# Attention inputs turned from the unscaled residual, with the inverse root applied as the projections leave PSUM

## The reference, cut to what matters

```
x  = x + rwkv7_time_mix(...)                     # ... @ w_out_a
kv = rms_norm(x, norm_kv) @ w_kv                 # k1, v1 (1024 columns each)
h  = rms_norm(x, norm_b);  proj = h @ w_in_b     # q1, gate g1 (1024 columns each)
k, q = partial_rope(rms_norm(k, k_norm)), partial_rope(rms_norm(q, q_norm))
o  = softmax(q k^T / 8, causal) v;   x = x + (o * silu(gate)) @ w_out_b
# rms_norm(x, g) = x * rsqrt(mean(x*x) + 1e-6) * g
```

## Time and profile before

| what | value |
| --- | --- |
| three runs, median (lowest to highest) | 1215.3 us (1212.01 to 1216.09) |
| the profiled execution | 1210.92 us, its span 1209.1 us |
| busy, share of the span: TensorE, VectorE, ScalarE | 92%, 60%, 41% |
| chain that ended last: TensorE, VectorE, ScalarE | 75%, 15%, 5% |
| mean granted TensorE clock | 0.977 of full |

### The profile page before, as it was taken

How to read it: one execution, slowest core, us unless ns; L and a number is a source line. 1 busy time by engine, 2 the same in 40 slices (tenths; PEclk the granted TensorE clock), 3 DMA queues, 4 the chain that set the end, 5 groups by cost and what they waited for, 6 DMA issues and landing times.

```text
span 1209.1 us, 19666 instructions
## 1 busy us (share of the span) xinstructions
PE 1113.5 (92%) x8524; PEld 900.8 (74%) x8524; DVE 730.5 (60%) x1128; ACT 501.2 (41%) x776; POOL 33.3 (3%) x30
## 2 busy tenths in 40 slices
PE   3999978898999988999998899999899699999997
PEld 2885468896768765777657699999567566998996
DVE  4671777856659956453566767667435736564544
ACT  3311313123454464345353455455233435555442
POOL 0000004400000010000000000000000000000000
PEclk9999989999999998999998999999999989999999
DMA  9373300520357450353332577866634445565520
GB/s 386 132 287 139 139 1 3 211 73 26 125 200 260 157 209 2 140 201 120 130 142 105 190 298 265 299 271 232 256 139 166 186 145 200 182 236 209 185 94 35
DMA packets 15078, 204.88 MB, mean 169 GB/s; under 512 B 1800, under 2 KB 1800, under 8 KB 2832
## 3 DMA queue, kind: packets, MB, share of 16 engines
q1 hardware_dynamic: 14256, 201.33, 44.4%
q10 hardware_dynamic: 736, 2.30, 0.5%
HBM read 202.57 MB, written 1.05 MB: 168 GB/s over the span
## 4 chain that ended last, share of the span: by engine, by line
PE 75%; DVE 15%; ACT 5%; DMA 3%; issue 2%; ACTq 0%; SPq 0%; DVEq 0%
PE bank L432 15%; PE bank L434 15%; PE bank L433 15%; PE bank L391 6%; PE bank L677 5%; PE bank L479 5%; PE bank L536 3%; DVE slot_parts L1727 3%; DMA ring<-in_stream 2%; PE bank L506 1%; ACT page_parts L1176 1%; DVE arena L1841 1%; PE bank L659 1%; ACT arena L1269 1%; DVE small L1701 1%
## 5 line engine op out<-in xcount | busy, mean ns | idle before, releaser
L432 PE MATMUL bank<-page_parts 128*128 128x512 f32 (+1 forms) x1152 | 394.1, 342 | 14.2 <-DVE page_parts L1760 9.5
L1727 DVE TENSOR_TENSOR slot_parts<-ring,page_parts 128x2048 fp32r<-128x2048 f32 x104 | 236.9, 2289 | 129.2 <-ACT page_parts L1176 128.9
L1176 ACT ACTIVATE page_parts<-ring 128x2048 fp32r<-128x2048 f32 x104 | 197.4, 1908 | 144.5 <-PE bank L434 97.5
L432 PEld LDWEIGHTS bank<-page_parts 128*128 128x128 f32 x1152 | 220.6, 191 | 39.8 <-issue 14.1
L434 PE MATMUL bank<-page_parts 128*128 128x512 f32 x576 | 227.1, 394 | 0.0
L433 PE MATMUL bank<-slot_parts,page_parts 128*128 128x512 f32 x576 | 227.0, 394 | 0.0
L1235 ACT ACTIVATE arena<-bank 128x512 f32<-128x512 f32 (+1 forms) x142 | 78.6, 570 | 223.8 <-PE bank L479 66.6
L433 PE MATMUL bank<-page_parts 128*128 128x256 f32 x576 | 163.2, 283 | 0.0
L434 PE MATMUL bank<-page_parts,slot_parts 128*128 128x256 f32 x576 | 163.2, 283 | 0.0
L434 PEld LDWEIGHTS bank<-page_parts 128*128 128x128 f32 x576 | 109.6, 190 | 23.4
L433 PEld LDWEIGHTS bank<-slot_parts,page_parts 128*128 128x128 f32 x576 | 110.1, 191 | 21.8
(11 more groups left out here) (272 smaller groups left out, 1155.1 us busy)
## 6 DMA issues: line engine op xcount, KB each, us to landing
ring<-in_stream SPq DMA_DIRECT2D x95, 2048.0 KB, 8.3
arena<-in_x SPq DMA_DIRECT2D x2, 512.0 KB, 6.3
gn<-in_gn ACTq DMA_DIRECT2D x2, 512.0 KB, 8.5
out<-arena SPq DMA_DIRECT2D x2, 512.0 KB, 2.6
cc<-in_consts ACTq DMA_DIRECT2D x1, 898.0 KB, 6.2
pc<-in_params ACTq DMA_DIRECT2D x1, 287.5 KB, 7.3
gn<-in_head_sel ACTq DMA_DIRECT2D x1, 32.0 KB
pos_i<-in_positions ACTq DMA_DIRECT2D x1, 1.0 KB, 7.1
```

Of the source, the lines that this page charges most:

```text
L432: mm(out, a[0], b[0], start=start, stop=False)
L1176: act(unit_parts(n)[0], unit_values(n)[1], ACT.Copy).then_inc(ac.step("w_hi"), 1)
L1727: tt(unit_parts(n)[1], lo, hi, ALU.subtract).then_inc(dv.step("w_lo"), 1)
```

## The change

TensorE turns X itself as soon as `add_to_x` has let each half go. ScalarE copies the eight tiles of `hkvT` first and then those of `hbT`, and forms the squares and the root afterwards. VectorE splits `hkvT`, one weight unit, `hbT`, and then forms the inverse root alone (no `XN` is written). ScalarE applies it, as a per-partition `scale`, in the 16 copies of k1, q1, v1 and g1. TensorE's direct panel there is gone; its columns are now a summed panel (eight VectorE operations) in the mLSTM stage, with its place in the order of loads after v2. The hunks below stand in the order TensorE, ScalarE, VectorE.

```diff
-            def transposes(name, src, tiles=KT, ready=None):
+            def transposes(name, src, tiles=KT, ready=None, added=None):
...
+                    if added:
+                        for tb in range(TB):
+                            pe.wait_ge(*evacuated((added, i // 2, tb)))
...
-            ada_direct()
-            pe.wait_ge(sem("xn"), 4)
-            transposes("hT_b", XN)
-            ada_turned()
+            transposes("hT_b", X, added="wo_a")
...
-                              wait=("hT_b_split", 0) if name == "k1" and half == 0 else None)
+                              wait=("hT_b_split", 4 * src) if name in ("k1", "q1") and half == 0 else None)
...
                 split_tok(("v2", half), split_parts(MLSTM_PAGES), first_of(6, 14, 11))
+            ada(1, rest=1)
             pe.wait_ge(sem("gate_rows"), 1)
...
-                               kw.get("func", ACT.Copy)).then_inc(ac.frees(product), 1)
+                               kw.get("func", ACT.Copy), scale=kw.get("scale", 1.0)).then_inc(ac.frees(product), 1)
...
             split(unit_of["k1", 0] + 1)
+            for dst, w, last in ((hkvT, "norm_kv", False), (hbT, "norm_b", True)):
+                for i in range(4):
+                    act_.wait_ge(*finished(("hT_b", i)))
+                    for jj in range(2):
+                        j = 2 * i + jj
+                        ins = act(dst[:, j, :], bank(("hT_b", i))[:, jj * T:(jj + 1) * T], ACT.Copy, scale=par(w)[:, j:j + 1])
+                        if jj == 0:
+                            ins.then_inc(ac.step(), 1)
+                        elif last:
+                            ins.then_inc(ac.frees(("hT_b", i)), 1)
+                        else:
+                            ins.then_inc(ac.step("hkv_left"), 1)
+            split(unit_of["k1", 0] + AHEAD)
             warm_root()
             x_squares("wo_a")
-            split(unit_of["k1", 0] + AHEAD)
-            ada_direct()
-            for i in range(4):
-                act_.wait_ge(*finished(("hT_b", i)))
-                for jj in range(2):
-                    j = 2 * i + jj
-                    for n, (dst, w) in enumerate(((hkvT, "norm_kv"), (hbT, "norm_b"))):
-                        ins = act(dst[:, j, :], bank(("hT_b", i))[:, jj * T:(jj + 1) * T], ACT.Copy, scale=par(w)[:, j:j + 1])
...
-            ada_turned()
+            act_.wait_ge(sem("x_scale"), 1)
...
-                        copy(dst[:, tb, half * 512:(half + 1) * 512], (name, half, tb), func=f)
+                        copy(dst[:, tb, half * 512:(half + 1) * 512], (name, half, tb), func=f, scale=ss[:, tb:tb + 1])
...
                     copy(V2[:, tb, 4 * half:4 * half + 4, 0:DV], ("v2", half, tb))
+            ada_columns()
...
-            def norm():
+            def norm(scale_only=False):
...
-                refined(ss, x_root, ss)
+                refined(ss, x_root, ss, "x_scale" if scale_only else None)
+                if scale_only:
+                    return
...
-                    dve.wait_ge(*evacuated((name, i)))
+                    dve.wait_ge(*(ready(i) if ready else evacuated((name, i))))
...
-            norm()
-
-            split_h("hT_b", HKV_PAGES, HB_PAGES)
-            for _ in range(4):
+            split_h("hT_b", HKV_PAGES, ready=lambda i: (sem("hkv_left"), i + 1))
+            next_unit(("k1", 0, 0))
+            split_h("hT_b", HB_PAGES)
+            norm(scale_only=True)
+            for _ in range(3):
                 next_unit(("k1", 0, 0))
             ada(KT)
...
                     modulation(4, 6, ())
                     gate_diagonal(0)
+            ada(KT)
             dve.wait_ge(sem("gate_ln"), 1)
```

More of the change, by code:

```diff
@@ L909, in mlp @@
                 stage[0] = f"mlp{l}"
-                pe.wait_ge(sem("xn"), 8 + 4 * l)
+                pe.wait_ge(sem("xn"), 6 + 4 * l)
                 transposes(f"hT_m{l}", XN)
@@ L957, in _ @@
             ada_direct()
-            pe.wait_ge(sem("xn"), 6)
+            pe.wait_ge(sem("xn"), 4)
             transposes("hT_c", XN)
@@ L1043, in _ @@
             ada_direct()
-            pe.wait_ge(sem("xn"), 10)
+            pe.wait_ge(sem("xn"), 8)
             transposes("hT_d", XN)
@@ L1647, in rsqrt, with refined @@
                     dve.wait_ge(*dv.last)
-            def refined(dst, root, square):
+            def refined(dst, root, square, to=None):
                 y, z = newton[:, 0, 0:TB], newton[:, 1, 0:TB]
@@ L1657, in refined @@
                 dve.wait_ge(*dv.last)
-                stt(dst, z, 1.5, y, ALU.add, ALU.mult).then_inc(dv.step(), 1)
+                stt(dst, z, 1.5, y, ALU.add, ALU.mult).then_inc(dv.step(to), 1)
                 dve.wait_ge(*dv.last)
             norms = [0]
-            def norm():
+            def norm(scale_only=False):
                 norms[0] += TB
@@ L1748, in split_output, with split_h @@
                 split(unit_of[name, 1] + 1)
-            def split_h(name, *buffers):
+            def split_h(name, *buffers, ready=None):
                 for i in range(4):
                     js = slice(2 * i, 2 * i + 2)
-                    dve.wait_ge(*evacuated((name, i)))
+                    dve.wait_ge(*(ready(i) if ready else evacuated((name, i))))
                     for n, pages in enumerate(buffers):
```

## The result

| | runs | median us | lowest to highest |
|---|---|---|---|
| kernel before, first series | 4 | 1215.69 | 1212.01 to 1216.68 |
| changed kernel, first series | 4 | 1204.73 | 1202.71 to 1205.61 |
| kernel before, second series | 23 | 1213.31 | 1209.71 to 1217.96 |
| changed kernel, second series | 6 | 1207.83 | 1202.81 to 1208.88 |
| kernel before, third series | 13 | 1212.94 | 1209.06 to 1216.76 |

The ratio to the kernel before is 0.9924 in the first series (95% interval 0.9897 to 0.995), 0.9949 in the second (0.9931 to 0.9968) and 0.9951 in the third (0.9933 to 0.9969): faster by 0.5 to 0.8%. Forecast were 1207.8 us and 7.5 us less; the medians fell by 11.0, 5.5 and 5.5 us. The execution whose profile follows took 1205.61 us, its span was 1203.8.

The account below looks back on a forecast made before the run. TensorE holds three quarters of the chain, but VectorE's arrival at the head norms ends the stage. 8.5 us gained there less 1.0 lost at og gives 7.5 off 1215.3: 1207.8 us, range 1203.5 to 1212.

Parts of the forecast that it names:

- the sum: Whole kernel: 8.5 us gained in the stage from wo_a to attention less 1.0 us lost at og, 7.5 us.
- k1's first product: Head of the stage after wo_a: TensorE starts k1 at 333.4, 10.1 us ahead of before.
- The third unit and the factor: Before k1's copies: VectorE starts k1's third unit at 339.15 and has the inverse root ready at 346.7.
- The stall at k1's fourth unit: In k1: that unit's split queues behind ScalarE's wait for the factor, so TensorE stalls 1.3 us.
- The stage: From wo_a to attention: ends 8.5 us earlier, carried by VectorE; bounds 7.1 and 8.8.
- The scale operand: ScalarE's 16 scaled copies of k1, q1, v1 and g1: cost nothing, at most 0.3 us.
- The moved panel's VectorE work: mLSTM stage: eight operations (5.91 us) fall into VectorE's idle time, costing nothing, or 5.9 us without that cover.
- Its load: mLSTM stage: og's second panel lands late, ScalarE waits 2.9 us; 1.0 us lost, ends at 0 and 2.1.
- Low clock at the two new restarts: Rival: clock falls before k1's fourth unit and before the mLSTM heads, 1.4 us each, 1210.6 us at worst; chance 0.12.
- a sign against it: mLSTM heads: the prediction counts as wrong if they lose more than 2.1 us.
- The attention stage at low clock: Rival: attention's products run at 0.50; at two thirds of the stretch 10 us lost, 1218 us; chance 0.04.
- everything shifts alike: Behind the mLSTM heads' start: the rest of the kernel only moves earlier, with no further gain or loss.

Follow-up runs that it names:

- e4: Changed kernel with ScalarE's split of k1's fourth unit ahead of its wait for the factor; 1204.49 us, ratio 0.994 to the kernel before.
- e3: Changed kernel with the mLSTM stage's summed panel ordered behind og's two panels instead of ahead; 1205.98 us, ratio 0.994 to the kernel before.
- e1: Changed kernel with the direct panel back on TensorE ahead of the transposes, only the unscaled turning kept; 1212.88 us, ratio 0.9998 to the kernel before.
- e2: Kernel before with only the direct panel moved, as a summed one, to the mLSTM stage, inputs still scaled before turning; 1215.18 us, ratio 1.0016.

## Why the prediction was right

The time (1204.73 to 1207.83 against 1207.8) came out, and the sum (7.5 predicted) lies between the 6.6 us of the mean times and the 8.1 us in span times clock. That two medians meet the forecast time to 0.4 us is partly luck: the kernel before had medians near 1213 in the later series and not 1215.3, and the gain in them was 5.5 us. Step by step:

- **k1's first product** was predicted 2.75 us after wo_a's last addition (333.4 - 330.65) and came after 2.67. ScalarE's first copy (0.55 predicted, 0.43), VectorE's first pair (1.42, 1.37) and hbT (6.45, 6.37) lie within 0.12 us.
- **The third unit and the factor.** From the first copy on, VectorE's unit was to start 7.95 us later (331.2 to 339.15) and took 7.78, the root's last operation was to end at 15.5 and ended at 15.07.
- **The stall at k1's fourth unit**: 1.3 us predicted, 0.62 measured. It is the mis-sized term. From ScalarE's first copy on, the unit was ready after 19.4 us (350.29 + 2.29 - 333.17; 19.8 summed), and TensorE came to it after 18.85 (352.64 - 0.62 - 333.17; 18.5 summed). It changed nothing, since VectorE sets the end.
- **The stage**: 8.5 predicted, 9.0 and 8.2 measured against the two profiles before. The sum was made against the first, and VectorE came to the head norm 0.6 us sooner than summed (30.98 after wo_a's last addition, 31.55 predicted). The prediction took the low clock at k1's head to cost 1.4 us of TensorE; the two profiles before differ by 0.8 at the head norm. That VectorE and not TensorE carries the gain is what e4 points to, and VectorE waits nowhere in the 40 us from the head norm on.
- **The scale operand**: nothing, at most 0.3 us. A copy takes 0.69 us; the mean of the others is 0.57. It stayed inside ScalarE's idle time.
- **The moved panel's VectorE work** was hidden, as said. **Its load** made ScalarE wait 2.10 us (2.9 predicted, the landing took 8.0 and not 8.7 us), VectorE was 1.4 late (2.1), and 0.7 was left at the heads (1.0), by the rotation. The load's part is shown by e3, where both the wait and the 1.4 us are gone. For a landing 0.7 us quicker the prediction had given 0.5.
- **Low clock at the two new restarts**: at k1's all nine profiles of kernels with this head show 0.47 us for the first product, and none the drop. In the heads it did come in some: the changed kernel's third profile has it at 570, and there the second head came 2.2 us late and not 0.7, just over the 2.1 that the prediction named as a sign against it.
- **The attention stage at low clock** (the rival for slower) did not occur in the changed kernel's profiles: 1.00 over its first 140 us in all three. It is the kernel before that had some of it in both of its profiles.
- **What the prediction left out**: anything behind the heads. It said that everything shifts alike; the profiles of the kernels with the moved panel are 3.4 to 7.3 us longer there (631.0 to 633.9 in ten, 626.6 to 627.6 in the three without it). The granted clock missing in that stretch is 15.0 to 20.0 us in the ten and 10.3 to 10.5 in the three, as much more as the stretch is longer. In the runs as a whole only 1.4 us of missing clock is to be seen, since the kernel before has a mean of 31.1 in its runs and 28 in its profiles. That the profiles with the moved panel are longer there is shown by e1 against e2 and the others; why is open. The load that mlp0's restart waits for landed after 8.1 to 8.5 us in the three and 8.4 to 9.7 in the ten; by which path it comes late, and why the clock falls, is not settled.

The rule of the Trainium skill that the prediction cited (TensorE: Matmul & The Clock Gate, Part 4: PE-mode transpose) could have let k1 begin at 1.2 GHz. In the changed kernel k1 began at full clock after 2.1 us of transposes and 0.78 of waiting. The rule would have changed nothing in the sum, and does not decide here: with 1.72 us of waiting the clock was down in one profile before and up in the other.

## What to carry to other kernels

- Two pieces of work that end beside each other must both go: each alone gave 1.0 to 3.1 us, together 8.2 to 9.0. In the runs neither alone was faster. Ask of each removed piece what would have been waited for without it.
- In a queue worked in order, try what a restart waits for ahead of what waits for a load: here it took 1.4 to 2.2 us off a wait, and the runs gained about 4.5 us in two series. The rest of that gain came as clock, at places that are not settled, and was not seen with other edits beside it.
- A panel moved in a ring of four, and a bank claimed earlier, are felt hundreds of us later. Compare stretches between marks that both kernels have, and split runs into span x clock and the missing clock before believing a difference of 3 us.

## What the hardware showed unexpectedly

- The granted clock at a restart did not follow the length of the wait: at the direct panel behind mlp0 it held after 3.43 us in three profiles out of three and fell after 2.17 in eight out of ten; at mlp0's restart it held after 2.4 to 2.9 us in four and fell after 3.1 to 3.9 in five, and after 1.7 it fell in three and held in one.
- The same load of 2048 KB, the one ahead of mlp0's restart, landed after 9.4, 9.7 and 8.9 us in three profiles of the changed kernel, with only the next load behind it in its queue, 7 us later in the first. In the kernel before, with the next load also 7 us behind, it took 8.1.
- Between runs of one kernel 24 to 38 us of granted clock were missing, and the slower runs are mostly those with more of it (correlation 0.8 over the 52 runs).
